# Thirty-two byte steps for the weight halves and the second activation buffer in a two-block transformer kernel

## What is computed

```python
proj = rmsnorm(x, attn_pre_g) @ w_in
x = x + rmsnorm(concat([o_nsa, o_swa]) @ w_o, attn_post_g)
a, u = split(rmsnorm(x, mlp_pre_g) @ w_gate_up)
x = x + rmsnorm((gelu(causal_dwconv(a)) * u) @ w_down, mlp_post_g)
x = x + (p @ w_ple) * sigmoid(x @ w_ple_gate)
proj = rms_norm(x, norm_mix_2) @ w_in_2
x = x + concat([na_out, ret_out]) @ w_out_2
x = x + square(relu(rms_norm(x, norm_mlp_2) @ w_up_2)) @ w_down_2
```

## Time and profile before

| | |
|---|---|
| median of 2 runs | 1295.58 us (1295.53 to 1295.63) |
| span of the profiled execution | 1293.9 us |
| TensorE busy in it | 1278.1 us, 99% |
| TensorE's weight loads | 1063.6 us, 82% |
| VectorE | 802.8 us, 62% |
| ScalarE | 635.7 us, 49% |
| GpSimd | 155.7 us, 12% |
| matmuls | 6136 |

### The profile page before, as it was taken

How to read it: one execution, slowest core, us unless ns; L and a number is a source line. 1 busy time by engine, 2 the same in 40 slices (tenths; PEclk the granted TensorE clock), 3 DMA queues, 4 the chain that set the end, 5 groups by cost and what they waited for, 6 DMA issues and landing times.

```text
span 1293.9 us, 16698 instructions
## 1 busy us (share of the span) xinstructions
PE 1278.1 (99%) x6136; PEld 1063.6 (82%) x6136; DVE 802.8 (62%) x1559; ACT 635.7 (49%) x1243; POOL 155.7 (12%) x146
## 2 busy tenths in 40 slices
PE   9999999999999999999999999999999999999998
PEld 8888888878888888888778777889888888888887
DVE  6699799685655565346788886578644343344334
ACT  6787576454335343234555655476543252342344
POOL 0022120000110011001002101022311030110111
PEclk9999999999999999999999999999999999999999
DMA  8211110433332333322323212432333323232321
GB/s 276 82 50 42 33 42 17 164 87 91 91 104 76 112 98 98 97 92 77 110 90 105 74 58 59 127 107 83 93 94 98 92 81 114 82 111 86 105 90 66
DMA packets 64624, 118.20 MB, mean 91 GB/s; under 512 B 7712, under 2 KB 12192, under 8 KB 64288
## 3 DMA queue, kind: packets, MB, share of 16 engines
q1 hardware_dynamic: 62704, 112.86, 28.7%
q10 hardware_dynamic: 1840, 4.29, 1.1%
HBM read 115.02 MB, written 2.10 MB: 91 GB/s over the span
## 4 chain that ended last, share of the span: by engine, by line
PE 87%; DVE 7%; issue 2%; ACT 2%; DMA 1%; POOL 0%; SPq 0%; POOLq 0%; DVEq 0%; ACTq 0%
PE bank L581 26%; PE bank L583 26%; PE bank L582 25%; PE bank L801 2%; PE bank L681 1%; PE bank L683 1%; PE bank L682 1%; DVE pp L2156 1%; PE bank L787 1%; PE bank L788 1%; DVE wl L1985 1%; DVE ptl L2178 1%; DVE pp L2173 1%; DMA raw<-in_w_swa 1%; DVE qs L2072 1%
## 5 line engine op out<-in xcount | busy, mean ns | idle before, releaser
L1985 DVE TENSOR_TENSOR wl<-raw,wh 128x512 fp32r<-128x512 f32 (+2 forms) x360 | 266.0, 750 | 326.6 <-ACT wh L1291 326.0
L1291 ACT ACTIVATE wh<-raw 128x512 fp32r<-128x512 f32 (+1 forms) x398 | 242.3, 619 | 287.6 <-PE bank L583 274.7
L581 PE MATMUL bank<-AH,wh 128*128 128x512 f32 (+1 forms) x848 | 333.0, 393 | 2.7 <-DVE AL L1999 0.8
L583 PE MATMUL bank<-AH,wl 128*128 128x512 f32 (+1 forms) x848 | 328.9, 388 | 0.0
L582 PE MATMUL bank<-AL,wh 128*128 128x512 f32 (+1 forms) x848 | 326.7, 385 | 0.0
L581 PE MATMUL bank<-BH,wh 128*128 128x512 f32 x624 | 248.4, 398 | 0.0
L583 PE MATMUL bank<-BH,wl 128*128 128x512 f32 x624 | 245.1, 393 | 0.0
L582 PE MATMUL bank<-BL,wh 128*128 128x512 f32 x624 | 243.8, 391 | 0.0
L581 PEld LDWEIGHTS bank<-AH,wh 128*128 128x128 f32 x848 | 159.5, 188 | 36.5 <-issue 4.0
L583 PEld LDWEIGHTS bank<-AH,wl 128*128 128x128 f32 x848 | 159.2, 188 | 35.3
L582 PEld LDWEIGHTS bank<-AL,wh 128*128 128x128 f32 x848 | 159.4, 188 | 33.0 <-issue 0.2
(11 more groups left out here) (336 smaller groups left out, 1632.0 us busy)
## 6 DMA issues: line engine op xcount, KB each, us to landing
raw<-in_w_dn SPq DMA_DIRECT2D x104, 256.0 KB, 2.6
raw<-in_w_gu SPq DMA_DIRECT2D x88, 256.0 KB, 2.6
raw<-in_w_up SPq DMA_DIRECT2D x64, 256.0 KB, 2.6
raw<-in_w_nsa SPq DMA_DIRECT2D x16, 256.0 KB, 2.6
raw<-in_w_pg SPq DMA_DIRECT2D x16, 256.0 KB, 2.7
raw<-in_w_naq SPq DMA_DIRECT2D x16, 256.0 KB, 2.6
nbi<-in_na_bias ACTq DMA_DIRECT2D x8, 448.0 KB, 3.3
raw<-in_w_swa SPq DMA_DIRECT2D x10, 256.0 KB, 3.0
```

What stands on the lines that cost most here:

```text
L581: t.matmul(o, w, xh, start=start, stop=False, skip_group_check=skip)
L583: return t.matmul(o, wl, xh, start=False, stop=stop, skip_group_check=skip)
L1291: a.activation(W[i % NW].h[:, 0:n], RAW[i % NRAW][:, 0:n], ACT.Copy).then_inc(*s_wh.up(i))
L1985: v.tensor_tensor(w.l[:, 0:n], RAW[i % NRAW][:, 0:n], w.h[:, 0:n], ALU.subtract).then_inc(*s_wl.up(i))
```

## The change

The ten weight halves are laid out with extra bytes in between, so that they begin 0, 32, 64, 96, 128, 160, 192, 224, 256 and 256 bytes behind where they stood relative to the first. The table of constants is cut from 256 to 192 columns, which gives back the 256 bytes: everything from a_dn to A stands where it did. Before B, 32 bytes are left out, so that B and all that is allocated behind it (the shared region of both blocks) stand 32 bytes further on. No instruction is added or removed.

```diff
--- before.py
+++ after.py
@@ -16,6 +16,7 @@
 EPS = 1e-6
 NEG = -1e30
 NW = 5
+W_AT = (0, 32, 64, 96, 128, 160, 192, 224, 256, 256)
 DOWN3_OUT = {7: (0,), 8: (1,), 9: (2,), 11: (3,), 12: (4,), 13: (5,), 14: (6,)}
 NRAW = 5
 N_UNITS = 28
@@ -275,18 +276,21 @@
         bank = Banks([ctx.enter_context(nc.psum_tensor(f"bank{i}", [P, 512], F32)) for i in range(8)])
 
         RAW = [new(f"raw{i}", 512) for i in range(NRAW)]
-        W = [Pair(new(f"wh{i}", 512, F32R), new(f"wl{i}", 512, F32R)) for i in range(NW)]
+        a_w, top[0] = top[0], top[0] + 4096 * NW + W_AT[-1]
+        halves = [at(f"w{'hl'[n % 2]}{n // 2}", 512, F32R, a_w + 2048 * n + W_AT[n]) for n in range(2 * NW)]
+        W = [Pair(halves[2 * i], halves[2 * i + 1]) for i in range(NW)]
         r_bc, r2_bc = new("r_bc", T), new("r2_bc", T)
         a_sq = region(1024)
         small = new("small", 128)
         ident = new("ident", P)
         ones = new("ones", P)
-        cst = new("cst", 256)
+        cst = new("cst", 192)
         a_dn = region(896)
         dn = at("dn", 512, F32, a_dn)
         ds = at("ds", 256, F32, a_dn + 2048)
         a_tmp = [new(f"tmp{i}", T + 2) for i in range(5)]
         aA = region(8192)
+        top[0] += 32
         aB = region(8192)
         AH, AL = at("AH", 4096, F32R, aA), at("AL", 4096, F32R, aA + 16384)
         BH, BL = at("BH", 4096, F32R, aB), at("BL", 4096, F32R, aB + 16384)
@@ -383,7 +387,7 @@
         def cc(n):
             a = c_used[0]
             c_used[0] += n
-            assert c_used[0] <= 256
+            assert c_used[0] <= 192
             return cst[:, a:a + n]
 
         g_pre, g_post, g_mpre, g_mpost, g2mix, g2mlp, g2fin = (cc(8) for _ in range(7))
```

## The result

The changed kernel takes 1305.68 us (median of 2 runs, 1305.65 to 1305.72) against 1295.58 before: the ratio is 1.0079, 95% interval 1.0049 to 1.0108. It is slower by 10.1 us, which is clear of the noise and under the 2% by which the prediction tells slower from same. The prediction had 1297 us within 1272 to 1320, so sign and range hold. But the loss is eight times what the forecast's sum gave (+1.2 us), and the time lies outside the forecast's own range of 1288 to 1304.

The account below looks back on a forecast made before the run. TensorE was taken to bound the kernel, through 4560 matmuls at 228.9 ns from start to start. The terms 0 + 0 + 0 + 1.2 gave +1.2 us on a 1293.9 us span, and with 1.7 us to the median 1297 us, range 1272 to 1320.

Parts of the forecast that it names:

- (a): Constants: the table shrinks from 256 to 192 columns, 177 of them used; 0 us.
- (b): Writers of the weight halves on ScalarE, VectorE and GpSimd, now at 32-byte residues: 0, between -0.1 and +0.1 us.
- (c): Transfers into B and behind it land 32 bytes off: 0 to +0.3 us, taken as 0.
- (d): Products with both operands behind B, such as attention scores, keep their relation to each other: 0 us.
- (f): Other engines' writes against TensorE's reads: new residues relative to the tiles being written buy nothing, 0 us.
- the prediction's signs: Its list of what would show each part right or wrong; (b) wrong if VectorE's subtractions are off 690 ns.
- rival 3: W products settle in the 233.3 ns state, +4.4 ns each: 1316 us, or 1326 if settling never ends; chance 0.20.
- (e): Relation of moving tile to weight half in TensorE's matmuls goes from one case to several; average stays, +1.2 us.
- The settling cost of 1.2 us: On TensorE, some 3 ns for each change of relation, at 398 weight pieces: 1.2 us.
- Rival 1: Bank conflict between moving tile and weights taken away, 15.6 ns off 2166 matmuls: 34 us less, 1262 us; chance 0.10.
- Rival 2: New relations settle TensorE's matmuls in a lower state, 2.2 ns below: -10 us, 1286 us; chance 0.12.
- Rival 4: Residues differ, but the store is interleaved by something the 32-byte steps don't touch: 1295.6 us; within the forecast's 0.58.

Follow-up runs that it names:

- e2: Kernel before with only the 32 bytes left out ahead of B, weight halves as before: 1301.62 us, ratio 1.0054.
- e10: Kernel before with all ten weight halves 128 bytes further on, distance 192 modulo 256: 1311.13 us.
- e13: Kernel before with all ten weight halves 96 bytes further on, distance 224 modulo 256: 1311.70 us.
- e3: Kernel before with all ten weight halves 64 bytes further on and the constants' table 64 bytes shorter, distance 0: 1285.80 us.
- e11: Kernel before with high halves at distance 0 and low halves 32 bytes beyond, at 224, in all five buffers: 1309.38 us.

## Why the prediction was right, and where it was wrong

The parts that held. The bound was rightly read: only the distance between two starts of the 4560 matmuls could move the time, at 4.56 us for each ns. (a), (b), (c), (d) and (f) came out at nothing: the busy time of VectorE went from 802.8 to 802.3 us, the taps kept their 744 and 740 ns, the other matmuls kept their time to some 0.5 us. (The 690 ns that the prediction's signs give for a subtraction is no row's: 756 ns before.) (f) is borne out by e2: B, into which results are written while A moves, stands 32 bytes off there, and A's 240 matmuls take 54.93 us as before.

That the range held is not to the mechanism's credit. It held because it was wide enough for most of rival 3, which had 0.20 of the chance; the forecast's own range missed, and its sign, +1.2 us, came from a cost that isn't what the time was lost to. The prediction's own test says so: it was right if 192 matmuls took 43.7 to 44.3 us with A as with B. By the windows after they take 44.5 us with A and 44.7 with B, near the 44.8 of rival 3.

The step that failed is (e), in the words "A start 32 bytes off shifts where they cross, not how often. Then the average stays". The average does not stay. Each distance that was run has a settled rate, between 226.7 and 233.3 ns, and the kernel before stood at the second best of the seven that were run. The settling cost of 1.2 us was beside the point (and read from rounded starts: in ns the triple of the earlier trace rows takes 697, not 690, some 10 ns over the steady 686.7); the true term was 2.91 ns for some 4450 matmuls, +12.9 us, of which 10.1 arrived. The changed kernel doesn't even settle: between halves at different distances its intervals wander from 224 to 241 ns, and only buffer 4 over A returns to the old three.

Two rows of the trace pointed to the answer. One is the earlier trace rows. I took its 233.3 ns for the same second state that the earlier trace rows shows, chosen by how a run begins, because modulo 128 the token products have the distance of all the others. Modulo 256 they have 192, and 233.3 ns is the rate of 192. That row said that an address may matter, and counting modulo 128 hid it. The other, a weaker one, is the earlier trace rows: at distance 0 modulo 256 the prediction read 230 ns twice, "not clearly faster", while the recorded starts of that pair are 227 and 227 ns apart (the other scores without a stop have 226 to 232). The view's steps of 10 ns covered the 2 ns that were to be seen. e10 shows the price: the products take 233.3 ns as soon as their distance is 192.

Rival 3 is what happened, in part: 231.8 and 232.7 ns lie 66% and 85% of the way from 228.9 to its 233.3. What it had wrong is the state: the changed kernel settles in no single one, and the 233.3 ns are no state chosen at the start of a run but, at most distances, the only rate there is. Its price of +20 us for all of it was the right size; e13 with every product at 233.3 lost 17.1 us against its own run of before (1294.63). Rival 1 was wrong in sign: it set the loss where the halves lie equal and freed those 32 bytes off, and e3 and e13 show that equal is best and 32 off worst. Rival 2 guessed the right size, 2.2 ns and 1286 us, for a state that the changed kernel doesn't reach and e3 does (226.7 ns, 1285.8 us). Rival 4 is dead.

Of the two pages of the Trainium skill: "SBUF — State Buffer" ("A bandwidth-pool intuition that's wrong (but worth ruling out)") has TensorE load weights through a second, independent port. The runs disagree: the same instructions take 226.7 or 233.3 ns according to the distance between the moving tile and the half that is loaded beside it. "TensorE: Matmul & The Clock Gate", again the Trainium skill ("Wait — 56ns, not 53.3ns?"), has 215.7 ns; no settled rate here is under 226.7, so 11 ns of that difference are not a matter of these addresses, as far as the distances that were run go.

What stays open is why the best distance still takes 13.3 ns more than 512 columns at 2.4 GHz, why 64 has two states (in the kernel before the 233.3 one holds, among others, in the 24 matmuls behind each of the two blocks of token products), and the law that gives 64 a better rate than its neighbours. That the two streams meet in the memory's banks is argued; shown is only that the distance decides, and that the long intervals begin with the load of the odd half and not with its use. Whether a mere change of distance costs something of its own (U' in e11) is open too.

## What to carry to other kernels

Where back-to-back fp32r matmuls of 512 columns are the bound, try laying the moving tiles and the weight tiles so that they begin at the same address modulo 256, all of them, both halves and every buffer; here the order of two allocations gained 0.75% with no byte spent, and staggering the tiles "against conflicts" lost 0.8%. Read the distance between starts of equal matmuls in every stage before and after a change of layout: two stages of one kernel with the same shapes and different rates (228.9 and 233.3 ns here) can be the sign that an address is at work. Take it from starts in ns, or over many matmuls: at 10 ns a step, two intervals don't tell 227 from 229. One load at a bad distance can spoil its neighbours' matmuls as well: in e11 one in three cost as much as all three.

## What was not expected of the hardware

- The rate of 512-column fp32r matmuls at the full clock depends on the distance between the moving tile and the next matmul's weights, with a period of 256 bytes as far as was run (that is, for distance 0): 226.7 ns at 0, 228.9 at 64, 232.4 at 128, 233.3 at 32, 96, 192 and 224.
- The averages lock in: 2720 ns for twelve at distance 0, 2800 ns at four distances whose patterns otherwise differ (at 192 intervals of 233 and 234 in most pieces, 231 and 236 in others; at 32 intervals of 231, 233, 234 and 235).
- The sign matters: 64 gave 228.9 ns in products and 192 gave 233.3. With the roles of the two tiles exchanged the rates were exchanged too, but for one block of 84 token matmuls which stayed at 233.3 at distance 64.
